# Seven half-size products in place of eight for the scan mixer's output projection, moved behind all four groups

## The chip, the cores and the metric

One core of a Trainium2 chip runs the whole program. The metric is the device time of one execution in microseconds (us); lower is better.

## The reference

A trunk of two layers on 1024 tokens of width 1024, all in float32. Layer 0 is windowed attention beside a pooling mixer, layer 1 is a Mamba-2 (SSD) mixer; a SwiGLU feed-forward network with 2816 hidden columns follows each. What the change touches is the end of the SSD mixer:

```python
y = ssd_chunked(xs, dt, A, Bm, Cm) + xs * D[:, None]        # 4 groups, 8 chunks of 128 tokens
y = y.reshape(b, s, 2048) * silu(z)                         # z = u @ w_in[:, :2048]
yg = y.reshape(b, s, 4, 512)
yg = yg * rsqrt(mean(yg * yg, -1) + EPS)                    # one mean for each token and group
y = yg.reshape(b, s, 2048) * norm_w
return y @ w_out                                            # 1024 x 2048 times 2048 x 1024
```

The result is added to the residual x, and `swiglu(rmsnorm(x))` comes next.

## The kernel before

The program is written by hand for each engine, in an order written out, with semaphores between the engines. PE is the matmul engine, DVE and POOL and ACT work on vectors, SP issues nearly all DMAs and waits in order.

**Matmul precision.** Each float32 product is three matmuls: an operand is split into a rounded part (`_hi`, copied by ACT) and the rest (`_lo`, a subtraction on DVE or POOL), and hi·hi, hi·lo and lo·hi are summed in a bank of PSUM. One such matmul has 128 rows of weights and 512 columns.

**Seven products.** The feed-forward layers, and the q stage that makes the inputs of the mixer, cut their matrices in four blocks and use seven block products (`M1` to `M7`) instead of eight, with sums of blocks made beforehand on DVE and POOL (`S1` to `S4`, `T1` to `T4`). The product that ends each FFN goes over slices: `down_slice(j, p)` is 12 matmuls for product j and row pair p; its operands come by DMA into a ring of 5 places (`s_val`, `d_val`), ACT makes the hi parts, POOL and DVE the lo parts, and `add_down` on DVE adds a finished bank to `xres` at one to four places.

**The SSD stage.** Four groups g, each of eight chunks c (`ssd_group`). Per chunk PE does `token_major` (a small product and transposes of rows read back from `conv_rows` into `bc_rows` and `yx`), `STATES`, `YOFF` and `YDIAG`; DVE masks the decays (`mdec`), updates the state and writes y into `yx`; ACT takes the exponentials; POOL scales (`xds`, `decayed`). Between chunks PE fills in `z_half` pieces (12 matmuls each, 16 in a group), which make the gate z. After the eight chunks the group's own output projection runs: y is multiplied by silu(z) (`gated`), squared, split in hi and lo with `norm_w` (`y_hi`, `y_lo`), and 16 outputs (8 token tiles, 2 column halves) of 4 row blocks each are computed with `out_part`, 192 matmuls. Since the mean is per token, and tokens lie on the partitions of the output, the factor 1/rms is applied by `add_out(rms)` on DVE when the bank is added to `xres`. The next group starts under the last outputs. In the last group the outputs go in the order `TILE_ORDER`, and the norm and the transposes (`ffn_T`) of the FFN behind are placed between them, tile by tile.

**FFN entry.** PE needs for its first products `M1g`, `M2g`, `M1u`, `M2u` only tiles 0 to 3; `M5g`, `M6g`, `M7g` need the block sums `T1`, `T2`, `T3` over tiles 4 to 7 (`tail_t1`, `tail_t2`, `tail_t3`, `tail_b22`, and then the lo parts `tail_lo1` to `tail_lo3` on DVE).

## Time and profile before

| | |
|---|---|
| median of 3 runs | 2283.26 us (2281.89 to 2283.43) |
| the profiled execution | 2282.14 us, of which the span of the trace is 2280.4 us |
| PE busy | 2258.5 us, 99% of the span |
| DVE, ACT, POOL busy | 1320.3, 1101.5, 1320.6 us |
| granted TensorE clock | 0.999 of full speed over the span |
| group of the SSD stage, scan and projection | 118.1 us |
| bytes by DMA | 281.45 MB, mean 123 GB/s |

Matmuls overlap, so a row's mean duration (390 ns for 128x512) is longer than the distance between two of them (227 ns); sums of PE work are made from distances.

### The profile page before, as it was taken

The page shows a single profiled execution, that of the slowest core. Times are in us where ns is not written, and L with a number is a line of the kernel's source. Part 1 is how long each engine was busy: PE and PEld are TensorE (multiplying, and loading weights), DVE is VectorE, ACT ScalarE, POOL GpSimd, SP SyncE. Part 2 cuts the span into 40 slices and gives each one's busy share as a digit, 9 for nine tenths or more (in the row PEclk, how much of TensorE's full clock was granted, in tenths as well). Part 3 has the DMA queues.
Part 4 walks back from the last instruction along what each step waited for, and adds up shares of the span by engine and source line. Part 5 has one row for each costly group of instructions (what it writes and reads, how often), then busy time and mean ns, then how long its engine had stood idle before and what let it go on. Part 6 is the DMA issues. An engine that isn't in the chain of part 4 may idle for free.

```text
span 2280.4 us, 28960 instructions
## 1 busy us (share of the span) xinstructions
PE 2258.5 (99%) x10698; PEld 1845.5 (81%) x10698; DVE 1320.3 (58%) x1716; ACT 1101.5 (48%) x2016; POOL 1320.6 (58%) x950
## 2 busy tenths in 40 slices
PE   8999999999999999999999999999999999999998
PEld 6877888888888878888878888888888888888887
DVE  7357663333335798855568484747854343336777
ACT  4046544333333446655567474737643333334445
POOL 3224288777774664787734242334388777774654
PEclk9999999999999999999999999999999999999999
DMA  5100323323227855233263323232222323228744
GB/s 164 47 28 19 120 64 112 120 88 120 88 102 259 268 161 166 93 112 119 86 222 123 120 84 118 86 102 93 102 88 97 122 84 122 85 106 292 250 148 155
DMA packets 170807, 281.45 MB, mean 123 GB/s; under 512 B 19232, under 2 KB 104108, under 8 KB 168108
## 3 DMA queue, kind: packets, MB, share of 16 engines
q1 hardware_dynamic: 167084, 267.68, 34.9%
q10 hardware_dynamic: 3584, 11.93, 1.3%
q8 instruction: 86, 1.41, 0.3%
q14 instruction: 53, 0.43, 0.1%
HBM read 209.71 MB, written 69.86 MB: 123 GB/s over the span
## 4 chain that ended last, share of the span: by engine, by line
PE 92%; DVE 3%; POOL 2%; issue 1%; ACT 1%; DMA 1%; SPq 0%; ACTq 0%; DVEq 0%; POOLq 0%
PE ps L2212 44%; PE ps L1925 8%; PE ps L1927 8%; PE ps L1926 8%; PE ps L2302 5%; PE ps L2306 5%; PE ps L2298 5%; PE ps L2592 1%; PE ps L2582 1%; PE ps L2575 1%; PE ps L1948 1%; PE ps L2370 1%; POOL sq L1205 1%; PE ps L2135 1%; PE ps L2168 1%
## 5 line engine op out<-in xcount | busy, mean ns | idle before, releaser
L1051 POOL TENSOR_TENSOR s_lo<-s_val,s_hi 128x512 fp32r<-128x512 f32 x154 | 235.5, 1533 | 196.7 <-ACT s_hi L1575 196.0
L2862 DVE TENSOR_TENSOR xres<-ps,xres 128x512 f32<-128x512 f32 x132 | 90.5, 688 | 400.2 <-PE ps L2212 400.2
L947 POOL TENSOR_TENSOR w_lo<-w_raw,w_hi 128x1024 fp32r<-128x1024 f32 x50 | 119.3, 2387 | 270.6 <-ACT w_hi L1239 205.9
L972 POOL TENSOR_TENSOR p_lo<-p_val,p_hi 128x512 fp32r<-128x512 f32 x176 | 239.4, 1369 | 48.6 <-ACT p_hi L1380 37.5
L1380 ACT ACTIVATE p_hi<-p_val 128x512 fp32r<-128x512 f32 x176 | 111.0, 632 | 307.8 <-POOL p_val L998 307.8
L2212 PE MATMUL ps<-xn_hi,p_hi 128*128 128x512 f32 x704 | 189.0, 390 | 1.2 <-ACT xres L1483 1.2
L2212 PE MATMUL ps<-xn_lo,p_hi 128*128 128x512 f32 x704 | 188.2, 389 | 0.0
L2212 PE MATMUL ps<-xn_hi,p_lo 128*128 128x512 f32 x704 | 188.2, 389 | 0.0
L1575 ACT ACTIVATE s_hi<-s_val 128x512 fp32r<-128x512 f32 x154 | 97.0, 630 | 160.8 <-DMA d_val<-in_w_down 89.9
L1925 PE MATMUL ps<-xn_hi,w_hi 128*128 128x512 f32 x400 | 160.3, 401 | 0.0
L1926 PE MATMUL ps<-xn_lo,w_hi 128*128 128x512 f32 x400 | 156.0, 390 | 0.0
L1927 PE MATMUL ps<-xn_hi,w_lo 128*128 128x512 f32 x400 | 155.9, 390 | 0.0
L2212 PEld LDWEIGHTS ps<-xn_hi,p_hi 128*128 128x128 f32 x704 | 131.5, 188 | 28.9 <-ACT p_hi L1380 2.0
L2212 PEld LDWEIGHTS ps<-xn_lo,p_hi 128*128 128x128 f32 x704 | 132.1, 188 | 27.5
L2212 PEld LDWEIGHTS ps<-xn_hi,p_lo 128*128 128x128 f32 x704 | 132.2, 188 | 27.5
L2302 PE MATMUL ps<-d_lo,s_hi 128*128 128x512 f32 x560 | 151.3, 390 | 1.0 <-DVE d_lo L2914 0.8
L2298 PE MATMUL ps<-d_hi,s_hi 128*128 128x512 f32 x560 | 151.0, 390 | 0.0
L2306 PE MATMUL ps<-d_hi,s_lo 128*128 128x512 f32 x560 | 150.7, 389 | 0.0
L2914 DVE TENSOR_TENSOR d_lo<-rows_v,d_hi 128x512 fp32r<-128x512 f32 x108 | 126.3, 1173 | 21.7 <-ACT d_hi L1578 21.6
L1483 ACT ACTIVATE xres<-ps 128x512 f32<-128x512 f32 x132 | 77.8, 591 | 113.8 <-PE ps L2212 113.8
L1239 ACT ACTIVATE w_hi<-w_raw 128x1024 fp32r<-128x1024 f32 x48 | 50.0, 1051 | 159.9 <-PE ps L1927 154.4
L2302 PEld LDWEIGHTS ps<-d_lo,s_hi 128*128 128x128 f32 x560 | 104.7, 188 | 24.6 <-DVE d_lo L2914 3.1
(361 smaller groups left out, 5570.3 us busy)
## 6 DMA issues: line engine op xcount, KB each, us to landing
s_val<-hidden SPq DMA_DIRECT2D x154, 256.0 KB, 2.9
hidden<-xres SPq DMA_DIRECT2D x20, 1792.0 KB, 6.5
wv_g<-in_w_gate SPq DMA_DIRECT2D x22, 1024.0 KB, 5.2
wv_u<-in_w_up SPq DMA_DIRECT2D x20, 1024.0 KB, 5.1
d_val<-in_w_down SPq DMA_DIRECT2D x70, 256.0 KB, 4.1
rows_v<-in_w_down SPq DMA_DIRECT2D x64, 256.0 KB, 3.8
mdec<-decay_sums SPq DMA_DIRECT2D x32, 512.0 KB, 4.2
xres<-parked_x SPq DMA_DIRECT2D x24, 512.0 KB, 6.0
```

Of the source, the lines that this page charges most:

```text
L947: pool.tensor_tensor(w_lo[piece.slot][:, :], raw[piece.raw][:, :], f(w_hi[piece.slot][:, :]), ALU.subtract).then_inc(lo_done, 1)
L972: pool.tensor_tensor(p_lo[n][:, :, :], src, f(p_hi[n][:, :, :]), ALU.subtract).then_inc(p_lo_done, 1)
L1051: pool.tensor_tensor(s_lo[i][:, :], s_val[i][:, :], f(s_hi[i][:, :]), ALU.subtract)\
L1380: act.activation(p_hi[n][:, :, :], src, ACT.Copy).then_inc(p_hi_done, 1)
L1925: pe.matmul(dst, l_hi, r_hi, start=first, stop=False, skip_group_check=reopened)
L1926: pe.matmul(dst, l_hi, r_lo, start=False, stop=False, skip_group_check=reopened)
L1927: return pe.matmul(dst, l_lo, r_hi, start=False, stop=last, skip_group_check=reopened)
L2212: ins = pe.matmul(bank, l_[:, k, :], r_[:, k, :], start=first and k == 0, stop=last and k == H2 - 1, skip_group_check=reopened)
L2298: pe.matmul(banks[t_], s_hi[i][:, t_ * P:(t_ + 1) * P], d_hi[i][:, :], start=p == 0, stop=False)
L2302: pe.matmul(banks[t_], s_hi[i][:, t_ * P:(t_ + 1) * P], d_lo[i][:, :], start=False, stop=False)
L2306: pe.matmul(banks[t_], s_lo[i][:, t_ * P:(t_ + 1) * P], d_hi[i][:, :], start=False, stop=False)\
L2914: dve.tensor_tensor(d_lo[i][:, :], down_operand(DOWN[j], p, i), f(d_hi[i][:, :]), ALU.subtract).then_inc(d_lo_done, 1)
```

## The change

The output projection of all four groups is taken out of the groups and done once behind the scans, as seven block products over 8 row pairs (56 slices, `out_slice`, 672 matmuls), in the manner of `down_slice`. For this:

- y must be normalized before the projection, since sums of blocks mix token halves. The squares are summed with the tokens along the free dimension (`square_sums` with the small matrix `pick`), ACT roots 4 rows, DVE inverts them, SP stores them to `rr_rows` and reads them back spread over all partitions (`root_row`), and DVE multiplies (`row_normed`). DVE then makes the block sums (`mix`, S1 to S4), and SP stores 14 blocks of 256 KB of each group to `gated_y` (`store_blocks`), from where `load_out` reads them slice by slice.
- This work of group g-1 stands inside the chunks of group g; that of the last group stands behind its scan. `yx` has two buffers. The rows of the next group are loaded in chunks 6 and 7 of the running one, and `token_major(k + 1)` runs across the border of groups.
- Two `z_half` pieces follow every chunk (in group 0, three stand ahead and one or two follow). No `out_slice` runs before the last scan ends. The order `OUT_SEQ` takes nine slices that don't need the last group first: six of M1 and three of M2.
- The residual x is read back from DRAM (`load_x_back`) and added with M1. The FFN entry of layer 1 is `second_entry`, with tiles in natural order: transposes of tiles 0 to 3 (`second_T`) between slices of M3, those of tiles 4 to 7 behind the projection.
- The q stage's semaphores are merged with those of the FFN products (names only).

The core of the diff, which stands for the same pattern elsewhere too:

```diff
+        OUT_SEQ = ([(0, p) for p in range(6)] + [(1, p) for p in range(3)] + [(0, p) for p in (6, 7)]
+                   + [(1, p) for p in range(3, NO)] + [(j, p) for j in range(2, 7) for p in range(NO)])
+        OUTS = len(OUT_SEQ)
...
+        Z_AFTER_CHUNK = [[(5,), (6, 7), (8,), (9,), (10, 11), (12, 13), (14,), (15,)],
+                         [(0, 1), (2, 3), (4, 5), (6, 7), (8, 9), (10, 11), (12, 13), (14, 15)],
+                         [(0, 1), (2, 3), (4, 5), (6, 7), (8, 9), (10, 11), (12, 13), (14, 15)],
+                         [(0, 1), (2, 3), (4, 5), (6, 7), (8, 9), (10, 11), (12, 13), (14, 15)]]
+        SILU_AFTER_CHUNK = [{1: (0, 1), 4: (2, 3, 4)}] + [{2: (0, 1), 4: (2, 3), 6: (4, 5)}] * (G - 1)
+        SILU_LATE = [(5, 6, 7)] + [(6, 7)] * (G - 1)
+        NEXT_PIECE = {6: 0, 7: 1}
+        LATE_PIECE = {0: 2, 1: 3}
...
+            def root_row(n):
+                sp.wait_ge(rms_ready, n + 1)
+                sp.dma_start(rr_rows[n], rinv[0:4, :]).then_inc(rr_stored, 16)
+                sp.wait_ge(rr_stored, 16 * (n + 1))
+                if n >= 2:
+                    sp.wait_ge(y_normed, BG * (n - 1))
+                if n:
+                    sp.wait_ge(rr_loaded, 16 * n)
+                sp.dma_start(rr[n % 2][:, :], rr_rows[n:n + 1].rearrange("a t l -> a (t l)").to_broadcast([P, BANK]))\
+                    .then_inc(rr_loaded, 16)
...
+                    if c == 6:
+                        if g:
+                            sp.wait_ge(y_normed, BG * 2 * g)
+                            store_blocks(g - 1, "M1", "M2")
+                            sp.wait_ge(mix_ready, 8 * (g - 1) + 4)
+                            store_blocks(g - 1, "M7")
+                        else:
+                            sp.wait_ge(gc_ready, 1)
+                        if not last:
+                            load_xrows(g + 1, 0)
+                            load_bc(g + 1, 0)
+                            load_piece(g + 1, 2)
+                    if c == 7:
+                        if g:
+                            sp.wait_ge(mix_ready, 8 * g)
+                            store_blocks(g - 1, "M6", "M3")
+                            sp.wait_ge(y_stored, 16 * 14 * g)
+                        if not last:
+                            load_xrows(g + 1, 1)
+                            sp.wait_ge(ydiag_full, NT * (g + 1))
+                            load_bc(g + 1, 1)
...
+            def out_loads(load_gate):
+                for s_ in range(2, 6):
+                    load_out(s_)
+                load_x_back(4)
+                load_out(6)
+                load_out(7)
+                load_x_back(0)
+                root_row(2 * G - 2)
+                load_x_back(5)
+                first_stores(G - 1)
+                sp.wait_ge(y_stored, 16 * (14 * (G - 1) + 4))
+                root_row(2 * G - 1)
+                load_out(8)
+                load_x_back(1)
+                sp.wait_ge(y_normed, BG * (2 * G - 1) + 2)
+                store_blocks(G - 1, "M1")
+                sp.wait_ge(y_stored, 16 * (14 * (G - 1) + 6))
...
+                load_out(9)
+                load_out(10)
+                load_x_back(6)
+                sp.wait_ge(y_normed, BG * 2 * G)
+                store_blocks(G - 1, "M2")
+                load_out(11)
+                load_x_back(2)
+                sp.wait_ge(mix_ready, 8 * (G - 1) + 4)
+                store_blocks(G - 1, "M7")
...
+            def square_sum(n):
...
+                        pool.wait_ge(m_ready, t.count("half", 2 * c + 2))
+                        lo(in_group(g + 1)(NEXT_PIECE[c]))
+                    if c == 1 and g:
+                        square_sum(2 * g - 1)
+                    if c == 5:
+                        square_sum(2 * g)
+                    if c >= 6 and g == G - 1:
...
+            def second_T(q):
+                pe.wait_ge(xn_ready, t.count("tile", 1))
+                if q < 2:
+                    pe.wait_ge(out_added, o_add_order.count(0, "M7", 2 * q + 1, 0, 1))
+                elif q == 4:
+                    pe.wait_ge(out_added, o_add_order.count(0, "M3", 1, 4, 1))
+                else:
+                    turn_free(1, {2: 0, 3: 1, 5: 2, 6: 4, 7: 5}[q])
+                transposed(turn_banks(1, q), xs_f[q % 2]).then_inc(turn_full, 1)
...
+            def out_slice(s_):
+                j, p = OUT_SEQ[s_]
+                n, i, banks = SLICES + s_ + 1, o_place(s_), out_banks(j)
+                if p == NO - 1:
+                    pe.wait_ge(s_lo_done, n)
+                    pe.wait_ge(d_lo_done, n)
+                    for t_ in range(4):
+                        mm3(banks[t_], os_hi[i][:, t_ * P:(t_ + 1) * P], os_lo[i][:, t_ * P:(t_ + 1) * P],
+                            od_hi[i][:, :], od_lo[i][:, :], False, True, True).then_inc(out_full, 1)
+                    return
+                pe.wait_ge(s_hi_done, n)
+                pe.wait_ge(d_hi_done, n)
+                for t_ in range(4):
+                    if p == 0 and j >= 2:
+                        pe.wait_ge(out_added, max(o_add_order.count(0, DOWN[j - 2], t_, first, half)
...
+                SUMS_AT = (3, 6) if last else (3, 7)
...
+                    if c in SUMS_AT:
+                        *first, final = Z_AFTER_CHUNK[g][c]
+                        for i in first:
+                            z_half(g, i)
+                        if c == 3 and g:
+                            square_sums(2 * g - 1)
+                        elif c == (6 if last else 7):
+                            square_sums(2 * g)
+                        z_half(g, final)
+                    else:
+                        for i in Z_AFTER_CHUNK[g][c]:
+                            z_half(g, i)
                 t.add("chunk", NT)
...
-                for n in range(2 * NT):
-                    if n == (2 * TILE_ORDER.index(4) if last else NT):
-                        pe.wait_ge(y_split, t.count("z", 2 * BG))
-                    out_part(n, [BG - 1] if n < EARLY_OUTS else range(BG)).then_inc(out_full, 1)
-                    if n in SSQ_AFTER_OUT[last]:
-                        square_sums(SSQ_AFTER_OUT[last].index(n))
-                    if last and n % 2 and n // 2 >= 2:
-                        ffn_T(1, n // 2 - 2)
-                t.add("z", 2 * BG)
...
+            for s_ in range(OUTS):
+                out_slice(s_)
+                if s_ == 3:
+                    square_sums(2 * G - 1)
+                if o_at(6, 2) <= s_ <= o_at(6, 5):
+                    second_T(s_ - o_at(6, 2))
...
+            def row_normed(g, b, h):
+                dve.wait_ge(rr_loaded, 16 * (2 * g + h + 1))
+                dve.wait_ge(sq_ready, BG * (2 * g + h + 1))
+                dve.scalar_tensor_tensor(half_of(g, b, h), half_of(g, b, h), gconst[:, g, GC_NW + b:GC_NW + b + 1],
+                                         rr[h][:, :], ALU.mult, ALU.mult).then_inc(y_normed, 1)
...
+                    masked_decay(c)
+                    if k + 1 < NT * G:
+                        token_major(k + 1)
+                    if c == 0 and g:
+                        gated(g - 1, 1)
+                        reciprocal_rms(2 * g - 2)
+                    if c == 2 and g:
+                        for b in range(BG):
+                            row_normed(g - 1, b, 0)
+                        for i in range(2):
+                            mix(g - 1, "S1", i)
+                    if c == 4:
+                        gated(g, 0)
+                        if g:
+                            reciprocal_rms(2 * g - 1)
+                    if c == 6 and g:
+                        for b in H1_ORDER:
+                            row_normed(g - 1, b, 1)
+                        for i in range(2):
+                            mix(g - 1, "S3", i)
+                    if c == 7 and g:
+                        for name in ("S2", "S4"):
+                            for i in range(2):
+                                mix(g - 1, name, i)
+                    if c >= 6 and last:
+                        out_low(c - 6)
...
+            gated(G - 1, 1)
+            reciprocal_rms(2 * G - 2)
+            out_low(2)
+            out_low(3)
+            for b in range(BG):
+                row_normed(G - 1, b, 0)
+            for i in range(2):
+                mix(G - 1, "S1", i)
+            out_low(4)
+            reciprocal_rms(2 * G - 1)
+            out_low(5)
+            for b in H1_ORDER:
+                row_normed(G - 1, b, 1)
+            for name in ("S3", "S2", "S4"):
+                for i in range(2):
+                    mix(G - 1, name, i)
+            ffn(1)
...
+                    for s_ in range(6, OUTS):
+                        j, p = OUT_SEQ[s_]
+                        if s_ + 1 < OUTS:
+                            out_sum(s_ + 1)
+                        if j == 6 and p in (5, 6):
+                            make(2 * p - 10)
+                            if p == 5:
+                                make(1)
+                        if (j, p) == (6, 7):
+                            make(3)
+                        out_low(s_)
...
+                            quota, limit = 8, "M1"
+                        elif j >= 2 and p in (0, 1):
+                            quota, limit = (4, "M1") if j == 2 else (0, "M1")
+                        elif 2 <= j <= 5 and p >= 3:
+                            quota, limit = 3, DOWN[j - 1]
+                        else:
+                            quota, limit = 0, "M1"
+                        for _ in range(quota):
+                            if taken < upto[limit]:
+                                add_result(*pending[taken])
+                                taken += 1
+                        if j == 6 and p in (3, 4):
+                            for t_ in (2 * p - 6, 2 * p - 5):
+                                add_result("M7", t_, 0, 0)
+                                add_result("M7", t_, 0, 1)
+                        if j == 6 and p >= 6:
+                            lo(p - 6)
...
+                    lo(2)
+                    lo(3)
+                    for t_ in range(4):
+                        add_result("M3", t_, 4, 1)
+                    for q in range(4, NT):
+                        make(q)
+                    for i in range(4):
+                        tail_t1(i)
+                        tail_t2(i)
+                        tail_t3(i)
+                        tail_b22(i)
+                    for i in range(4):
+                        tail_lo1(i)
+                    for i in range(4):
+                        tail_t4(i)
+                        tail_lo2(i)
+                    for i in range(1, 4):
+                        tail_lo3(i)
...
```

## Rows read from the trace of the kernel before

**Rows 1.** The page, part 1: busy us of each engine.

```profile
PE 2258.5 (99%) x10698; PEld 1845.5 (81%) x10698; DVE 1320.3 (58%) x1716; ACT 1101.5 (48%) x2016; POOL 1320.6 (58%) x950
```

**Rows 2.** Waits of PE over the span: us in total, times, longest.

```profile
PE ps L2606 <- POOL sq L1205: 1.6, 3, 0.5
```

**Rows 3.** Chain in order of time: token transposes of chunk 0, two groups.

```profile
1285.27 0.44 PE ps L2544 x4
...
1403.41 0.44 PE ps L2544 x4
```

**Rows 4.** PE timeline, FFN down projection of layer 0: one slice to the next.

```profile
858.31 1.07 PE L2298 MATMUL ps<-d_hi,s_hi 128*128 128x512 f32 x4
...
861.03 1.07 PE L2298 MATMUL ps<-d_hi,s_hi 128*128 128x512 f32 x4
```

**Rows 5.** PE timeline, one chunk of group 1, to the next chunk's start.

```profile
1324.27 0.38 PE L2537 MATMUL ps<-bc_rows 128*128 128x128 f32 x2
...
1326.88 1.09 PE L2592 MATMUL ps<-mdec,xdt 128*64 128x128 f32 x16
1333.47 0.38 PE L2537 MATMUL ps<-bc_rows 128*128 128x128 f32 x2
```

**Rows 6.** Busy us by window inside group 1's scan: PE, PEld, DVE, ACT, POOL.

```profile
1320.00:1340.00 20.00, 20.00 (x123) 16.26 (x122) 15.70 (x32) 14.54 (x35) 8.23 (x7) 1.00 0.32 99
```

**Rows 7.** Groups by line and shape on POOL, the same stretch.

```profile
L1205 POOL TENSOR_TENSOR sq<-sq,sq 128x512 f32<-128x512 f32 x6 | 9.3, 1543 | 16.9 <-ACT sq L1871 16.5
```

**Rows 8.** Timeline of SP's queue at a group's start: DMA issues.

```profile
1400.39 0.33 SPq L856 DMA_DIRECT2D mdec<-decay_sums  x1
...
1401.24 0.47 SPq L804 DMA_DIRECT2D yx<-conv_rows  x1
```

**Rows 9.** DMA issues, 1398 to 1408 us: KB each, us to landing.

```profile
yx<-conv_rows SPq DMA_DIRECT2D x1, 1024.0 KB, 7.5
...
bc_rows<-conv_rows SPq DMA_DIRECT2D x1, 512.0 KB, 5.4
```

**Rows 10.** DMA issues over the whole span: KB each, median us to landing.

```profile
s_val<-hidden SPq DMA_DIRECT2D x154, 256.0 KB, 2.9
...
d_val<-in_w_down SPq DMA_DIRECT2D x70, 256.0 KB, 4.1
...
conv_rows<-xres SPq DMA_DIRECT2D x24, 512.0 KB, 3.3
...
decay_sums<-sumT ACTq DMA_DIRECT2D x1, 128.0 KB, 2.4
```

**Rows 11.** DVE timeline, entry of the second FFN.

```profile
1649.09 0.68 DVE L2766 TENSOR_TENSOR t_val<-ps,comb_val 128x512 f32<-128x512 f32 x1
...
1651.60 0.68 DVE L2766 TENSOR_TENSOR t_val<-ps,comb_val 128x512 f32<-128x512 f32 x1
...
1653.40 1.28 DVE L2791 TENSOR_TENSOR xn_lo<-t_val,xn_hi 128x512 fp32r<-128x512 f32 x2
...
1658.81 4.81 DVE L2803 TENSOR_TENSOR comb_lo<-comb_val,comb_hi 128x512 fp32r<-128x512 f32 x3
```

**Rows 12.** DVE timeline, last product of layer 0's down projection.

```profile
889.20 2.47 DVE L2926 TENSOR_TENSOR xres<-ps,xres 128x512 f32<-128x512 f32 x4
...
894.77 1.56 DVE L2691 SCALAR_TENSOR_TENSOR xs_n<-xres,small,norm_wp 128x1024 f32<-128x1024 f32 x1
```

**Rows 13.** PE timeline, the same product: its first slice, the first transpose.

```profile
883.33 1.07 PE L2298 MATMUL ps<-d_hi,s_hi 128*128 128x512 f32 x4
...
896.93 1.04 PE L1948 MATMUL ps<-ident,xs_n 128*128 128x128 f32 x8
```

**Rows 14.** Busy us by window, layer 0's down projection (columns as in rows 6).

```profile
822.00:852.00 30.00, 29.25 (x125) 22.74 (x124) 30.00 (x32) 13.81 (x23) 19.78 (x12) 1.00 0.43 127
```

More of the change, by code:

```diff
@@ new lines, in ssd_group @@
+                for c in range(NT):
+                    if NT * g + c + 2 < NT * G:
+                        load_decay(NT * g + c + 2)
+                    if c == 0 and g:
+                        root_row(2 * g - 2)
+                    if c == 1 and not last:
+                        load_piece(g + 1, 0)
+                    if c == 2 and g:
+                        first_stores(g - 1)
+                    if c == 2 and not last:
+                        load_piece(g + 1, 1)
+                    if (g, c) == (0, 3):
+                        store_row(row_at(NQ - 1, "g", 1))
+                        store_row(row_at(NQ - 1, "g", 2))
+                    if c == 3 and last:
+                        load_out(0)
+                    if c == 4 and g:
+                        sp.wait_ge(y_stored, 16 * (14 * (g - 1) + 4))
+                        root_row(2 * g - 1)
+                    if (g, c) == (0, 5):
@@ L901, in ssd_group @@
[L901 to L906 removed]
+                    if c == 5 and last:
+                        load_out(1)
+                    if c == 6:
[10 more added lines that the diff above has]
+                            load_piece(g + 1, 2)
@@ L2222, in product @@
                         if mn == "M1g":
-                            turn_free(layer, 4)
+                            turn_free(layer, 3 if layer else 4)
+                        elif mn == "M1u" and layer:
+                            pe.wait_ge(out_added, o_add_order.count(0, "M3", 3, 4, 1))
                         elif mn == "M1u":
@@ new lines, in z_half @@
+            def z_half(g, i):
+                n = i // 2
+                u, (b, half) = ZU * g + n, Z_ORDER[g][n]
+                piece = in_group(g)(b)
+                if i % 2 == 0:
+                    if b not in [b_ for b_, _ in Z_ORDER[g][:n]]:
+                        pe.wait_ge(lo_done, piece.count(1))
+                    if u >= 3:
+                        pe.wait_ge(z_done, u - 2)
+                ins = columns(z_bank(u), piece, half, range(i % 2 * NK // 2, (i % 2 + 1) * NK // 2))
+                if i % 2:
+                    ins.then_inc(z_full, 1)
@@ new lines, in token_major @@
+            def token_major(k):
+                g, c = k // NT, k % NT
+                tok = slice(c * P, (c + 1) * P)
+                if c % 4 == 0:
+                    pe.wait_ge(rows_loaded[c // 4], 32 * (g + 1))
+                if k:
+                    pe.wait_ge(cb_freed, k)
+                if c == 5 and g:
+                    pe.wait_ge(rms_rooted, 2 * g)
+                elif c == 1 and g:
+                    pe.wait_ge(rms_rooted, 2 * g - 1)
+                ins = pe.matmul(ps[:, CB, 0:P], BT[:, tok], CT[:, tok], start=True, stop=True)
+                if c < NT - 1:
+                    ins = pe.transpose(ps[:, CB, P:2 * P], BT[:, tok], ident[:, :])
+                ins.then_inc(cb_full, 1)
+                if k:
+                    pe.wait_ge(xdt_ready, k)
+                for b in range(BG):
+                    ins = pe.transpose(ps[:, XS, b * P:(b + 1) * P], yx[g % 2][:, b, tok], ident[:, :])
+                ins.then_inc(xsT_full, 1)
@@ new lines, in square_sums @@
+            def square_sums(n):
+                pe.wait_ge(sq_summed, n + 1)
+                if n == 2 * G - 1:
+                    pe.wait_ge(ydiag_read, NT * G)
+                else:
+                    g = n // 2 + n % 2
+                    pe.wait_ge(cb_freed, NT * g + 5 if n % 2 else min(NT * (g + 1) + 1, NT * G))
+                for tt in range(4):
+                    ins = pe.matmul(ssq_rows(n), pick[:, 4 * tt:4 * tt + 4], sq[0][:, tt * P:(tt + 1) * P],
+                                    start=tt == 0, stop=tt == 3, skip_group_check=True)
+                ins.then_inc(ssq_full, 1)
```

1178 lines of the change are left out of this document (681 added, 497 removed), and 2 rows, old and new, of the table comb_hi_order.

## The prediction

> **What bounds the kernel now.** I read the page's busy shares first: PE is busy 99% of the span, the others 48% to 58% [rows 1]. Busy time counts overlapping matmuls, so the next view was the list of waits: at the group ends of the SSD stage PE waits only 1.6 us in all, for POOL's sum of squares [rows 2]. The timeline then gives PE's real rate: a slice of 12 matmuls comes every 2.72 us (858.31 to 861.03), so one matmul costs 0.2267 us [rows 4]. The chain in order of time gives the group: 1403.41 - 1285.27 = 118.14 us [rows 3]. The reader is to see that PE is the bound everywhere and that there is nearly no slack: what PE no longer does is won, and every wait put in front of it is lost. So the question is whether the new order still hides its dependences.
>
> **What is removed.** The projection falls from 4 x 192 = 768 matmuls to 56 x 12 = 672: 96 x 0.2267 = 21.8 us off PE, at the same form of matmul, so I give this term no other bounds. The group ends, now without a stop between scan and projection, give back the 1.6 us of [rows 2] and little more; I take 2 us (0 to 4: a group's matmuls, 384 x 0.2267 = 87.1, and eight chunks of 9.20 - 24 x 0.2267 = 3.76 us, 30.1 [rows 5], leave about 1 us of the 118.1). Transposes and z pieces stay as many. Gain: 24 us.
>
> **Cost A, the border between groups.** `token_major(k + 1)` now stands at the head of chunk 7 and wants the next group's rows. SP issues them in chunk 6, behind `load_decay(8g + 8)`, which waits for chunk 6's YDIAG. Behind that YDIAG PE has two z pieces, 24 x 0.2267 = 5.4 us, and then nothing. Before, the same trio (mdec, bc_rows, yx) took from 1400.39 to 1401.24 + 7.5 = 1408.7, 8.35 us [rows 8, 9]. So group 0 costs 2.9 us. In groups 1 and 2 SP waits longer, for four `row_normed` and two `mix` of the group before. From chunk 6's start DVE comes to them at about 1.8 us (an estimate: PE's transposes end at 1.0 and `xdt` takes one operation more), six operations take 0.6 us each when alone (1.28 for two) and 1.6 when POOL is active (4.81 for three) [rows 11]; at 0.9 they end at 7.2. Six stores go out meanwhile, some 0.35 us of issue each [rows 8], then the rows: issued at about 8.5, behind 1.5 MB of stores, landed at about 15.2. PE is there at 9.2 [rows 5]: 6 us, twice. A = 2.9 + 12 = 15 us (10 to 20, with the operations at 0.6 and 1.6 us). Queued behind PE's wait is all of chunk 7, and DVE, ACT and POOL wait with it, so they don't make up for it.
>
> **Cost B, the start of the projection.** Count from chunk 7 of group 3. PE: YDIAG to 3.5, two z pieces to 8.9, then slices at 2.72 and one `square_sums` of 0.9; unhindered it needs the DVE part of slice 6 (`out_low(6)`) at 8.9 + 0.9 + 6 x 2.72 + 0.9 = 27. What has to happen before, since DVE keeps its order and SP its own: masks and four mixes (5.5); four stores issued (7) and landed, 3.3 us [rows 10] (10), for which SP waits; 14 loads issued at 0.33 to 0.47 us [rows 8] (15.4), whose 4 MB arrive, at the pace of [rows 8, 9] less one latency, by 22 to 23; behind them in the same queue the first `rr_rows` store and its load back, 2.4 to 2.9 us each [rows 10] (25.6); four `row_normed`, two mixes (30.5); four stores and their landing (35); the second `rr_rows` store and load (40.2); then `row_normed` x4 and `mix` x6 at 0.7 us (47) and only then `out_low(6)` (47.7). Slice 4 waits on the way for the first half of the chain, which changes nothing of the end. B = 47.7 - 27 = 21 us. Low end, every DMA at 2.4 and every operation at 0.6: 15. High end, 4.1 (the slice loads of [rows 10]) and 1.6: 28. Slice 9 needs M1's last stores, back at about 50 and wanted at 55: hidden behind slices 6 to 8.
>
> A DMA's landing in [rows 10] runs from 2.4 us for 128 KB to 4.1 for 256 KB in a busy queue. The Trainium skill, "DMA: Bandwidth & Descriptors", section "Anatomy of one DMA — SWDGE (gpsimd) path", says that each DMA pays about 2.0 us fixed besides its bytes at 436 GB/s. It speaks against this change, which strings seven dependent DMAs before slice 9; by it (an estimate from that page) they cost 14 us fixed, and B would be near its low end, where the traces' prices give 21.
>
> **Cost C, the FFN entry.** Three places. First, `second_T(0)` stands behind slice 3 of M3, 8.2 us after its start. In layer 0 the like transpose stood five slices behind, 883.33 to 896.93, with no wait [rows 13]; DVE made the M7 adds from 5.9 us on, and the norm began 11.4 us after the start and took 1.56 [rows 12, 13]. The adds stand one slice earlier now; the norm ends at about 12: 4 us. Second, T6 follows T5 on PE directly, but needs the banks of T4, and DVE frees these (four operations, 1649.09 to 1651.60 = 2.5 us [rows 11]) only after `make(7)` (1.3 us), which waits for T5: 4 us. Third, from there DVE has 3 x 2.5 us more of such sums, four `tail_lo1`, eight of `tail_t4` and `tail_lo2` (0.6 alone), then three at 1.6; PE has M1u, M2u and one transpose between, 6.3 us, and M5g and M6g wait for their low parts: 4 us (1 to 9). Before, outputs stood between the tiles and this work was hidden; now only products of tiles 0 to 3 cover it. C = 12 us (8 to 17).
>
> **Cost D, DVE and POOL inside the scans.** A scan lasts 8 x 9.2 = 73.6 us of PE. DVE was busy 15.70 of 20 us there [rows 6], 58 us a scan, and gets 16 operations more: 10 us at 0.6, 26 at 1.6. So it lies between 68 and 84 of 73.6: hardly hidden. POOL's sum of squares (3 x 1.54 = 4.6 us [rows 7]) now stands ahead of `xds` of chunk 2, about 1 us too late. In the projection, slices with sums, low parts and three adds fill DVE wholly; in layer 0 such a stretch cost PE 0.75 of 30 us [rows 14]. I take 4 us together (0 to 20), near the low end, since the waits of A give DVE time to catch up.
>
> [Rows 11] show 0.6 us for a DVE subtraction from SBUF alone and 1.6 beside POOL. The Trainium skill, "SBUF — State Buffer", section "SBUF: two separate sides", calls the pair of ports shared by the two an exclusive lock held for a whole instruction. If that struck all 16 operations, DVE would be the bound of the scans, which is the third rival.
>
> **Sum.** -24 + 15 + 21 + 12 + 4 = +28 us on the profiled span of 2280.4: 2308.4. That execution took 2282.14, 1.7 us beside its span, and the median of the runs is 1.1 above it: 2311 us. With the ends of the terms the four costs are 33 to 85 us and the gain 22 to 26, so the time lies between 2290 and 2346 if the mechanisms hold; I take the middle of most, since their ends are independent and none of the rows favours one side.
>
> **Rivals.** (1) All is hidden and PE stays the bound: 2283.3 - 24 = 2259 us. For it: [rows 2] show a kernel whose order hides its waits; PE has 33 us of work from the last YDIAG to slice 9. Against: nothing stands on PE behind the z pieces at the group border. It decides if A, B, C and D together stay under 24 us, which asks above all that the chain of B fit into 27 us. Chance 0.10. (2) B is hidden, because small DMAs overtake the bulk loads and DVE's order fits; A, C and D remain: 2283.3 + 7 = 2290. Chance 0.15. (3) DVE becomes the bound of the scans, 84 instead of 73.6 us in the three groups with the new work: 2311 + 3 x 10 = 2341. Chance 0.07. That fewer matmuls are not run is no rival: the loops count them.
>
> **Numbers.** My forecast, all four costs, has 0.68, with a range of its own of 2297 to 2326. What a measurement can tell here from no change is 0.2%, 4.6 us. Rival 1 and its edge give faster 0.12; the edge between rivals 1 and 2 gives same 0.05; slower 0.83. The range, 2288 to 2329, holds rival 2 and leaves out rivals 1 and 3 and the tails.
>
> **What would show it.** In the trace of after: 672 matmuls in the projection; PE idle before the transposes of `yx` (or the product before them) once in each of groups 0 to 2, released by the row DMAs, 3, 6, 6 us; PE idle in the early slices, released by DVE's low parts, some 20 us in all; idle before three to four matmul groups and transposes at the FFN entry, released by DVE, 12 us; DVE above 85% in the scans. I am wrong if the rows are landed when chunk 7 begins, or if DVE reaches `out_low(6)` before PE has done slice 5.

## The result

Median after 2365.2 us (2363.2 to 2367.9, 4 runs), before 2282.9 (2281.9 to 2283.4, 4 runs beside them): ratio 1.0362, 95% interval 1.0344 to 1.0380. The change costs 82 us. The prediction had the direction (slower, 0.83) and far too little of it: 2311 us, with 2329 as the upper end.

### The profile page after: what moved, and what is told of

It is laid out like the page before. It is cut to its first block, busy times and chain, and to the rows that moved or that the text cites. A ratio compares the mean times of both kernels' runs of the same rounds, so it can differ in the third digit from the quotient of the medians.

```text
span 2366.2 us, 29286 instructions
## 1 busy us (share of the span) xinstructions
PE 2267.5 (96%) x10602; PEld 1842.8 (78%) x10602; DVE 1425.7 (60%) x1828; ACT 1147.5 (48%) x2101; POOL 1369.6 (58%) x992
## 4 chain that ended last, share of the span: by engine, by line
PE 84%; DVE 7%; DMA 3%; issue 2%; POOL 2%; SPq 1%; ACT 1%; DVEq 0%; ACTq 0%; POOLq 0%
PE ps L2525 43%; PE ps L2228 5%; PE ps L2230 5%; PE ps L2229 5%; PE ps L2617 5%; PE ps L2621 5%; PE ps L2613 5%; PE ps L2909 1%; PE ps L2913 1%; PE ps L2905 1%; PE ps L2251 1%; PE ps L2974 1%; PE ps L2694 1%; DVE yx L3791 1%; DMA bc_rows<-conv_rows 1%
## 5 line engine op out<-in xcount | busy, mean ns | idle before, releaser
L1143 POOL TENSOR_TENSOR w_lo<-w_raw,w_hi 128x1024 fp32r<-128x1024 f32 x34 | 81.7, 2406 | 197.3 <-ACT w_hi L1471 114.6
L2525 PE MATMUL ps<-xn_hi,p_hi 128*128 128x512 f32 x704 | 190.8, 393 | 1.9 <-ACT xres L1765 1.3
L2525 PE MATMUL ps<-xn_lo,p_hi 128*128 128x512 f32 x704 | 189.7, 392 | 1.4 <-DVE xn_lo L3145 1.4
L2525 PE MATMUL ps<-xn_hi,p_lo 128*128 128x512 f32 x704 | 188.2, 389 | 0.0
L2525 PEld LDWEIGHTS ps<-xn_lo,p_hi 128*128 128x128 f32 x704 | 133.2, 189 | 29.7 <-DVE xn_lo L3145 1.8
L2525 PEld LDWEIGHTS ps<-xn_hi,p_hi 128*128 128x128 f32 x704 | 132.6, 189 | 30.2 <-ACT p_hi L1616 3.1
L2525 PEld LDWEIGHTS ps<-xn_hi,p_lo 128*128 128x128 f32 x704 | 132.3, 188 | 27.6
L1397 POOL TENSOR_TENSOR os_lo<-os_val,os_hi 128x512 fp32r<-128x512 f32 x56 | 89.6, 1607 | 104.7 <-ACT os_hi L2135 104.6
L2617 PEld LDWEIGHTS ps<-d_lo,s_hi 128*128 128x128 f32 x560 | 104.7, 188 | 25.6 <-DVE d_lo L3331 4.2
```

Of the source, the lines that this page charges most:

```text
L2525: ins = pe.matmul(bank, l_[:, k, :], r_[:, k, :], start=first and k == 0, stop=last and k == H2 - 1, skip_group_check=reopened)
L2617: pe.matmul(banks[t_], s_hi[i][:, t_ * P:(t_ + 1) * P], d_lo[i][:, :], start=False, stop=False)
```

## The profile after

The page of the kernel after, parts 1 and 2 (busy us; then the granted clock in 40 slices), beside [rows 1]:

```profile
span 2366.2 us, 29286 instructions
PE 2267.5 (96%) x10602; PEld 1842.8 (78%) x10602; DVE 1425.7 (60%) x1828; ACT 1147.5 (48%) x2101; POOL 1369.6 (58%) x992
...
PEclk9999999999999999999999899889989999999999
```

The 96 matmuls are gone (10698 to 10602). PE's idle time rose from 2280.4 - 2258.5 = 21.9 us to 2366.2 - 2267.5 = 98.7, by 76.8. And its busy time rose by 9.0 us although 21.8 us of work had left it. The last row says why: the clock, 0.999 over the span before and 0.982 now, shows an 8 in four slices from the 23rd to the 30th. So there are two things to read here: the waits, and what they do to the clock.

PE's waits in the kernel after, from the first scan to the first products behind the projection (us in total, times, longest), beside [rows 2]:

```profile
PE ps L2864 <- DMA bc_rows<-conv_rows: 20.6, 3, 7.6
PE ps L2909 <- DVE od_lo L3747: 16.9, 2, 9.4
PE ps L2974 <- DVE mdec L3835: 10.7, 7, 2.1
PE ps L2905 <- DVE xres L3761: 7.4, 3, 3.1
PE ps L2525 <- DVE comb_lo L3151: 7.2, 1, 7.2
PE ps L2251 <- DVE xn_lo L3135: 4.1, 1, 4.1
PE ps L2957 <- POOL xds L1426: 2.6, 3, 0.9
```

L2864 is `token_major` (cost A), L2905 and L2909 are `out_slice` (B), L2525 and L2251 products and `second_T` (C), L2974 and L2957 YDIAG and STATES in the scans (D). With the smaller rows they are 20.6, 27.2, 16.5 and 13.3 us, 77.6 in all.

The same kernel by windows: four in a row around one wait for rows, then one stretch of lowered clock each in the scans, in the projection and at the FFN entry (PE, PEld, DVE, ACT, POOL busy, granted clock, DMA share, GB/s):

```profile
1227.00:1232.00 5.00, 5.00 (x37) 3.87 (x35) 3.87 (x10) 2.78 (x6) 0.49 (x1) 1.00 0.38 84
1232.00:1235.34 3.34, 0.04 (x1) 0.00 (x0) 0.47 (x1) 1.54 (x6) 2.34 (x1) 1.00 0.95 325
1235.34:1242.17 6.83, 4.30 (x23) 4.08 (x25) 1.87 (x4) 3.33 (x7) 1.04 (x1) 0.50 0.49 167
1242.17:1250.00 7.83, 7.83 (x60) 5.80 (x57) 4.92 (x11) 5.92 (x8) 1.53 (x1) 1.00 0.73 252
...
1392.35:1395.77 3.42, 3.42 (x10) 2.68 (x9) 3.35 (x9) 3.11 (x5) 1.64 (x2) 0.50 0.41 153
...
1542.54:1552.78 10.24, 5.86 (x14) 4.65 (x15) 7.34 (x12) 2.36 (x5) 8.63 (x3) 0.50 0.77 236
...
1716.62:1723.45 6.83, 5.17 (x17) 4.42 (x18) 6.57 (x11) 4.09 (x8) 1.27 (x1) 0.50 0.42 173
```

PE stops at 1232, the clock goes from 2.4 to 1.2 GHz at 1235.3 while it is still idle, PE starts again at 1237.9, and full clock comes back at 1242.2. In between 4.3 us of work ran at half speed; about 2.2 of them are lost behind a wait of 5.8. There are eleven such stretches, 78.6 us, with PE busy for 50.7 of them: half of that, 25.3 us, is lost. By place: rows 14.0 us busy, so 7.0 lost; scans 10.3 and 5.1; projection 16.3 and 8.2; entry 10.1 and 5.0. The Trainium skill, "TensorE: Matmul & The Clock Gate", section "What's actually happening", calls the halved clock the default that activity releases; the rows agree with its two levels and with its direction.

The sum on the spans: -21.8 (matmuls) + 76.8 (idle) + 25.3 (clock) = +80.3; measured 85.8. About 2.0 of the other 5.5 us are the eight `square_sums`, which have a new form: PE takes 1.29 us from the last z matmul ahead of one to the first behind it (1281.96 to 1283.25), where the sums of before took 1.03 (1596.79 to 1597.82). The last 3.5 us are not explained. They are not a matter of the waits: PE's busy time less half of its work at the lower clock is 2241 to 2244 us in the traces of all 14 kernels behind the change (in e3_fill less the 20.4 us of its fill), whether PE stood for 58 us or for 103.

PE's timeline at the start of the projection (start, us, instruction, in brackets the idle time before it and its releaser):

```profile
1531.87 2.07 PE L2909 MATMUL ps<-od_lo,os_hi 128*128 128x512 f32 x4 [9.40 <-DVE od_lo L3747]
...
1546.92 2.08 PE L2909 MATMUL ps<-od_lo,os_hi 128*128 128x512 f32 x4 [7.55 <-DVE od_lo L3747]
...
1584.32 0.79 PE L2905 MATMUL ps<-od_hi,os_hi 128*128 128x512 f32 x1 [3.10 <-DVE xres L3761]
```

DVE at the same place:

```profile
1525.55 4.34 DVE L3802 SCALAR_TENSOR_TENSOR yx<-yx,gconst,rr 128x512 f32<-128x512 f32 x4 [8.79 <-DMA rr<-rr_rows]
...
1539.92 2.74 DVE L3802 SCALAR_TENSOR_TENSOR yx<-yx,gconst,rr 128x512 f32<-128x512 f32 x4 [6.70 <-DMA rr<-rr_rows]
```

And SP's queue:

```profile
1515.22 0.50 SPq L939 DMA_DIRECT2D rr_rows<-rinv  x1
1521.56 0.33 SPq L945 DMA_DIRECT2D rr<-rr_rows  x1
```

The low part of slice 4 stands on DVE behind the first four `row_normed`, which wait for the row's round trip: stored at 1515.2 behind 14 loads, back at 1525.5. That is the first wait; slice 6's is the second; M1's adds, which DVE reaches late, the third.

## The experiments

Each is the kernel after with one edit, unless it says otherwise. Differences are of medians; by the intervals of the ratios such a difference is uncertain by some 5 us, so for the small ones (e8, e6, and e1, whose highest run is as slow as the kernel after) the waits in the trace carry the verdict.

**e3_fill: the clock alone.**

```
+ if c == NT - 1 and not last:
+     pe.wait_ge(xdt_ready, k + 1)
+     for _ in range((26, 32, 32)[g]):
+         pe.matmul(ps[:, XS, :], xn_hi[:, 0, 0:P], xn_hi[:, 0, 0:BANK], start=True, stop=True)
  token_major(k + 1)
```

> At the three borders between groups TensorE is idle for the rows for 5.8, 7.2 and 7.6 us. Here 26, 32 and 32 matmuls of the z pieces' form (0.2267 us each, 5.9, 7.3 and 7.3 us) run in that wait, into the bank that the transposes write next; their result is overwritten, and nothing of the computation is left out. Theory (a wait costs its own length and then half of the work that runs at the lower clock after it): the granted clock stays at 1.0 there; in the three stretches at half clock TensorE was busy for 4.57, 6.35 and 3.92 us, half of it comes back, 7.4 us: 2358 us (2355 to 2361). Rival (after the wait DVE, ACT or DMAs set the pace, so the clock costs nothing): 2365 us, with the clock at 1.0 all the same. Second rival (the clock does not depend on TensorE's idle time): the three stretches stay at half clock, 2365 us or more.

2359.1 us, 6 less (7.4 expected), ratio 1.0326 (1.0311 to 1.0341). By windows:

```profile
1232.00:1238.00 6.00, 5.29 (x27) 4.17 (x26) 0.05 (x1) 4.89 (x11) 1.61 (x1) 1.00 0.92 327
1238.00:1245.00 7.00, 7.00 (x56) 5.84 (x55) 5.10 (x12) 3.51 (x6) 1.04 (x1) 1.00 0.47 147
```

The rows come when they came before, PE has nothing more useful to do, and the kernel is faster: the clock stays at 1.00 at all three borders. The wait's second price is real. Its size at the borders is less sure, since more changed than was aimed at: in this trace two of the three short stretches in the scans are gone too, with the same waits for masks (10.7 us), and 24 us of PE's work ran at the lower clock where after had 50.7.

**e2_rows_pe and e1_rows_sp: cost A from PE's side and from SP's.**

```
  # PE (and DVE, behind the y sums)
- if k + 1 < NT * G: token_major(k + 1)                  # head of every chunk
+ if k + 1 < NT * G and c < NT - 1: token_major(k + 1)
+ ... z_half(g, 14); if c == NT - 1 and not last: token_major(k + 1); square_sums(2 * g); z_half(g, 15)
```

> The first token_major of the next group is moved from the head of chunk 7 to behind its YDIAG and first z piece, on TensorE and on DVE (behind the y sums). SP's order is unchanged, so the rows land as before, 5.8 to 7.6 us after chunk 7 begins; TensorE comes to them at 3.8 + 2.7 = 6.5 us. Theory (cost A is a wait with nothing in front of it, plus the clock): of 20.6 us idle 2 remain, and 7.4 us of half clock go too; up to 1 us a border for DVE's copies before the sum of squares comes on: 20.6 - 2 + 7.4 - 3 = 23 us less, 2342 us (2338 to 2348). Rival (the wait moves: xds and states of chunk 0 are late by what token_major is later): 2355 to 2365 us, idle before STATES and YDIAG of chunk 0.

```
+ if c == 5 and not last: load_bc(g + 1, 0)
  if c == 6: wait y_normed, mix_ready
-     store M1, M2, M7; load_xrows(g + 1, 0); load_bc(g + 1, 0)
+     load_xrows(g + 1, 0); store M1, M2, M7
```

> SP's order alone: the B and C rows of the next group are issued in chunk 5, and the x rows in chunk 6 ahead of the stores of M1, M2 and M7 instead of behind them. Theory of the prediction (rows are behind six stores' issue, 2.1 us, and their 1.5 MB, in groups 1 and 2, and behind DVE's row_normed and mixes, which stay): the waits for rows fall from 20.6 to about 12 us, the clock gives back 3: 2354 us (2349 to 2359). Rival (DVE's operations ahead of the stores are all of it): waits stay at 17 or more, 2361 us or more. In group 0, which has no stores, both expect 1 us or so, since only the B and C rows come earlier.

e2 2347.9 us, 17 less (23 expected); e1 2358.5, 7 less (11). In e2's waits of PE the rows fell from 20.6 to 6.8, of which group 0 alone has 5.0: `Z_AFTER_CHUNK` gives it one piece behind chunk 7 and not two, so the moved `token_major` has none in front of it there. The masks took some back:

```profile
PE ps L2974 <- DVE mdec L3837: 14.0, 9, 2.1
...
PE ps L2864 <- DMA bc_rows<-conv_rows: 6.8, 3, 5.0
```

e1's waits for rows fell to 13.8. So two things are shown to set cost A, how much work stands ahead of PE's wait, and SP's stores ahead of the loads, the first for more.

**e4_spread and e8_spread_pool: cost D.** DVE's new operations in halves over two chunks:

```
- if c == 0 and g: gated(g - 1, 1); reciprocal_rms(2 * g - 2)
+ if c == 0 and g: gated(g - 1, 1, (0, 1)); reciprocal_rms(2 * g - 2)
+ if c == 1 and g: gated(g - 1, 1, (2, 3))
  ... likewise row_normed over chunks 2 and 3, gated(g, 0) over 4 and 5
```

> DVE's added operations inside the scans are halved over two chunks: gates in chunks 0 and 1 and in 4 and 5, row_normed in 2 and 3, the first stores in chunk 3. The number of operations is the same. Theory (cost D is lumps of 4 to 6 us ahead of a mask, not too much work in all: DVE is idle 6 us at every border and 3 us in chunks between): waits of YDIAG and STATES fall from 13.3 to about 4 us, and the three stretches of half clock beside them (3.41 us each, all busy) give back 5: 2351 us (2347 to 2356). Rival (DVE is the bound of the scans): the waits only move, 2362 us or more.

2371.6 us, 6 more. The theory failed; PE's waits in the scans show where the time went:

```profile
PE ps L2957 <- POOL xds L1426: 15.2, 3, 5.1
PE ps L2974 <- DVE mdec L3835: 0.6, 1, 0.6
```

The mask waits went as expected. But POOL's `square_sum` of chunk 1 now waited for the gates of chunk 1, and behind it in POOL's queue stood `xds` of chunk 2. e8 moves it (`- if c == 1 and g: square_sum(2 * g - 1)`, `+ if c == 2 and g: ...`).

> e4_spread again, and POOL's sum of squares of the second half moved from chunk 1 to chunk 2, behind its xds. In e4_spread the 10.7 us of waits for masks fell to 0.6, and 15.2 us of waits for xds came, 5.1 us once in each of groups 1 to 3, where POOL stood in the sum of squares and waited for the gates that now come in chunk 1. Theory (D is lumps in DVE's and POOL's order, not too much work): both kinds of wait go, under 3 us stay, 10 us less idle than after and 5 us less of half clock: 2350 us (2346 to 2355). Rival (DVE has too much work, the wait finds another place): 2360 us or more.

2361.2 us, 4 less than after and 10 less than e4: the xds waits are gone, but three mask waits of 2.7 us (8.0 us) are there, as the rival had it (2360 or more, the wait finds another place). DVE's timeline ahead of one:

```profile
1350.80 5.72 DVE L3899 SCALAR_TENSOR_TENSOR yx<-yx,gconst,eacs 128x128 f32<-128x128 f32 x4
1356.44 2.35 DVE L3835 TENSOR_TENSOR mdec<-mdec,cbm 128x512 f32<-128x512 f32 x2
```

POOL's:

```profile
1355.06 4.87 POOL L1405 TENSOR_TENSOR sq<-sq,sq 128x512 f32<-128x512 f32 x3
```

The four y sums take 5.72 us here.

**e11_small_sums: is it POOL?** e8_spread_pool with `- sq[0][:, :]`, `+ sq[0][:, 0:8]` in POOL's sums, which leaves the squares of most columns out.

> e8_spread_pool with POOL's sums of the squares made over 8 of 512 columns, so that the norm is not the reference's; left out are 21 POOL operations of 1.5 us. In the trace of e7_all, which has the same order, the four y sums beside these POOL operations took 5.72 us instead of 1.14. Theory (the mask waits of 2.7 us in each of groups 1 to 3 come from POOL holding DVE up, not from the number of DVE's operations): 8.5 us of waits fall to under 1.5, 3 us of half clock go with them: 2361 - 10 = 2351 us (2347 to 2355), and the y sums there take 1.2 to 2 us. Rival (DVE's own lumps make the wait): 2358 us or more.

2352.8 us, 8 less than e8 (10 expected); the mask waits fell from 8.0 to 1.8. The part on the y sums was wrong:

```profile
1344.86 4.71 DVE L3899 SCALAR_TENSOR_TENSOR yx<-yx,gconst,eacs 128x128 f32<-128x128 f32 x4
1349.49 1.28 DVE L3835 TENSOR_TENSOR mdec<-mdec,cbm 128x512 f32<-128x512 f32 x2
...
1355.85 1.14 DVE L3899 SCALAR_TENSOR_TENSOR yx<-yx,gconst,eacs 128x128 f32<-128x128 f32 x4
```

The y sums still took 4.71 us, beside POOL's `w_lo`, `xds` and `decayed`; what the sums of squares had added is 1.0 us there and 1.1 on the masks. In the next chunk, with POOL idle, they took 1.14. The sums of squares were enough to make the waits, but they are only a part of what POOL does to DVE.

**e9_mask_first: the mask ahead of the y sums.** `masked_decay(c + 1)` moves on DVE in front of chunk c's y sums.

> After, with one move on DVE: the mask product of chunk c + 1 stands ahead of the four y sums of chunk c instead of behind them; nothing else changes. Theory (D: DVE is only late at the mask that YDIAG waits for, by lumps of at most 2.1 us that the y sums of 1.1 to 5.7 us can take instead): the 10.7 us of waits for masks fall under 3, xds stays at 2.6, and half of the three stretches of 3.4 us at half clock comes back: 2365 - 8 - 5 = 2352 us (2348 to 2358). Rival (the mask product then waits for ACT's exponentials, or ACT waits for the y sums): 2363 us or more.

2355.5 us, 10 less (13 expected): mask waits 10.7 to 3.2, xds 2.6 to 1.5. Alone it is the best repair of D, and its trace has no stretch of lowered clock in the scans but those behind the waits for rows.

**e5_proj: cost B.**

```
- OUT_SEQ = [(0, 0..5), (1, 0..2), (0, 6), (0, 7), (1, 3..7), ...]
+ OUT_SEQ = [(0, 0..5), (1, 0..5), (0, 6), (0, 7), (1, 6), (1, 7), ...]
  # SP: rr_rows stored ahead of load_out(6), load_out(7); load_out(8) ahead of first_stores
  # DVE: out_low(4) ahead of the first row_normed, out_low(5) to out_low(11) between the norm's operations
```

> The start of the projection: twelve slices of groups 0 to 2 instead of nine come ahead of the first that needs the last group; the row of reciprocal roots is stored before the loads of slices 6 and 7, slice 8 is loaded ahead of the second row's round trip, and DVE splits slices 4 to 11 between the norm's operations instead of behind all of them. The work is the same. Theory (cost B is the order, DVE's low part of slice 6 and the loads of 8 and up behind the chain): of 27.2 us of waits between 1515 and 1610 us some 6 stay (slice 12 some 2 us late, slice 14 and the adds another 4), and of the three stretches at half clock (17.1 us busy in them, 8.6 lost) 7 come back: 2365 - 28 = 2337 us (2331 to 2345). Rival (the chain of seven dependent DMAs is longer than any cover, and the wait moves to slice 12): 2350 us or more.

2358.4 us, 7 less where 28 were expected; the rival (2350 or more) holds. PE's waits of the projection:

```profile
PE ps L2238 <- DVE od_lo L3757: 9.4, 2, 7.5
PE ps L2915 <- DVE xres L3771: 5.1, 2, 3.1
```

From 27.2 only to 20.2 us. The wait moved to slice 15: DVE makes its low part behind the sum of slice 16, and SP loaded slice 16 behind the last stores' landing.

**e6_entry: cost C.** DVE's order: `make(7)` behind the tails of tile 4, three `tail_t4` ahead of `tail_lo1`.

> DVE's order at the FFN entry alone: the sums of tile 4 come before the norm of tile 7 instead of behind it, and three of the four T4 subtractions (1.75 us each beside POOL) move from in front of the low parts that M6g waits for into the gaps before and between the tiles. Theory (cost C is order): T6's wait of 4.1 us goes, M6g's of 7.2 us falls to 2, and of the 5.3 us that the two stretches at half clock cost 4 come back: 2352 us (2348 to 2357). Rival (DVE's work between M3's adds and M6g's low parts is the bound, in whatever order): M6g waits as much longer as T6 waits less, 2362 us or more.

2359.7 us, 5 less (13 expected): waits 16.5 to 12.0. T6's 4.1 fell to 0.5, but M5g now waits 2.4 and 3.1 for parts that came late, M6g 2.8. DVE is busy without a gap from M3's adds to M6g's low part, so both were half right: the order mattered for 4 us, the rest is DVE's work.

**e7_all, e10_all2, e12_all3: together.** e7 is e1, e2, e8, e5 and e6, with group 0's x rows in chunk 5 too; e10 adds e9 and loads slices 16 and 17 ahead of the wait for the last stores; e12 has those loads without e9.

> All together: the rows' loads ahead of the stores and the first token_major behind a z piece (in group 0 the x rows in chunk 5 too), the spread gates and norms with POOL's sum behind xds, the projection's start and the FFN entry. Theory (the four costs are independent waits in TensorE's order, each with its half clock): rows 28 us, scans 15, projection 28, entry 13, together 84 of the 82 us: 2283 us (2275 to 2296), the granted clock 1.0 but for one or two stretches, TensorE idle under 35 us. Rival (the costs share DVE, and what one gives the next takes): 2305 us or more.

> e7_all with the mask product ahead of the y sums, and with the loads of slices 16 and 17 ahead of the wait for the last stores. In e7_all 12.3 us of waits for masks, 3.1 us for the sum of squares behind the rows and 8.4 us for the low part of slice 15, which DVE makes behind the sum of slice 16, were left. Theory: masks under 3 us, slice 15 under 2, and 7 us of half clock: 2327 - 9 - 7 - 7 = 2304 us (2298 to 2312), still slower than before, with the entry and DVE's pace beside POOL left. Rival (DVE is the bound of the scans in this order): 2318 us or more, with waits of the same sum elsewhere.

> e7_all with the loads of slices 16 and 17 ahead of the wait for the last stores, and without the mask product's move, which made e10_all2 slower by making DVE wait 25.1 us for ACT's exponentials. Theory: of e7_all's 8.4 us for the low part of slice 15, which DVE makes behind the sum of slice 16, 4 go, and 4 us of half clock in the projection; the adds' waits stay: 2327 - 7 = 2320 us (2315 to 2325). Rival (the loads only move the wait to the adds): 2326 us or more. No theory has it faster than before (2283).

e7 2327.5 us, e10 2337.8, e12 2323.0: ratios 1.0196, 1.0241 and 1.0187 (1.0171 to 1.0203). e7 missed its forecast of 2283 by 45 us and e10 its 2304 by 34; both lie where their rivals put them. e12 is in its range, but its five runs reach from 2322.6 to 2330.2 and e7's four from 2326.1 to 2330.2, so that it is faster than e7 isn't shown. The single repairs give 7 + 17 + 4 + 7 + 5 = 40 us, e7 38. So e7's rival had the number, but hardly the reason: the gains add up, and what is missing was missing in each repair alone, which together gave under half of the 90 us of their expectations. It is no proof that the costs are independent (e7 has one edit more, and e1 and e2 go for the same wait), and e9 shows that they are not wholly so, since it stops paying there. Waits of DVE in e10's scans:

```profile
DVE mdec L3859 <- ACT mdec L2187: 25.1, 12, 4.0
```

In e9 this was 14.7 us, and there PE stood for rows for 21.6 us, in which the others could catch up; that this hid it is my reading, which no run isolates. No version beats the kernel before: e12 is 40 us behind it. Its PE is idle for 2321.2 - 2258.7 = 62.5 us, 40.6 more than before, and 33.5 us of its work ran at half clock, 16.7 lost: 40.6 + 16.7 - 21.8 = 35.5 of the 40.8 on the spans.

**e13_light_dve: is it DVE?** e12 with `row_normed` and POOL's sums over 8 columns in the scans.

> e12_all3 with row_normed over 8 of 512 columns in groups 0 to 2 and POOL's sums of squares over 8 of 512, so that the norm is left out for most columns; DVE is spared 24 operations of 0.65 to 1.2 us and POOL 24 of 1.5. Theory (in the best order DVE, busy for 218 of 235 us of the scans in e7_all, is the bound there): the waits for masks and for DVE's copies, 15.4 us, fall under 3, with the half clock of the scans (6.8 us): e12_all3 less 15 us, 2305 us (2300 to 2311). Rival (the order, ACT or the DMAs bound the scans): at most 5 us less than e12_all3.

2317.1 us, 6 less than e12: nearer the rival's 5 than the theory's 15. Most columns stay without the norm here, and both DVE and POOL are spared. The scans by window, of e12:

```profile
1245.00:1480.00 235.00, 220.73 (x1326) 174.97 (x1325) 215.29 (x344) 183.40 (x364) 102.83 (x67) 0.97 0.43 147
```

and of e13:

```profile
1245.00:1480.00 235.00, 226.73 (x1367) 180.08 (x1366) 192.99 (x356) 184.82 (x367) 74.85 (x68) 0.99 0.46 156
```

DVE falls from 92% busy to 82% and PE gains 6 us: the mask waits go (12.3 to 2.7 us), while DVE waits 16.0 us for ACT and PE 7.1 instead of 3.1 at the borders. So DVE, with POOL beside it, was the nearest bound of the best order, and ACT comes right behind it; which of the two mattered more, e13 doesn't separate.

## Why the prediction failed

| term | forecast | waits measured (gain: matmuls) | lost to the clock |
|---|---|---|---|
| gain | -24 | -21.8 | |
| A, borders | 15 (10 to 20) | 20.6 | 7.0 |
| B, start of projection | 21 (15 to 28) | 27.2 | 8.2 |
| C, FFN entry | 12 (8 to 17) | 16.5 | 5.0 |
| D, scans | 4 (0 to 20) | 13.3 | 5.1 |
| sum | +28 | +56 | +25 |

The four mechanisms were right: the main waits are at the places and from the engines that were named, and the repairs of each gave time back. The sum failed at two steps, and either alone would have left the measured time above the stated 2329: with the waits as measured and no clock it comes to some 2339 us, with the waits as forecast and the clock to some 2336.

**A term was missing.** The sum priced a wait at its length. The clock before was 0.999, since PE never stood for more than 1.6 us in all at these places [rows 2], so none of the rows showed what a stop does; that was a reason to ask, not to leave it out. The trace of before does hold one fall of the clock, at its very end, where it costs nothing: PE's last matmul ends at 2273.1 us, and from 2276.5 on the granted clock is 0.50. The clock took 25 us, nearly a third of the result; e3_fill shows that it is paid for the stop itself.

**All four costs were too small, D by three times.** Each lies in the upper half of its range or just above it. "I take the middle of most, since their ends are independent" failed with them: four ends that are missed on the same side add up.
- A: in groups 1 and 2 the forecast gave 6 us each, measured 7.2 and 7.6; the rows were issued at 1317.53, 9.2 us into chunk 6, where I had 8.5. Group 0 was forecast at 2.9 and took 5.8. The DMAs were not the reason: from the issue of `mdec` at 1229.16 to the landing at 1237.8 they took 8.6 us, forecast 8.35. The step that failed is "PE has two z pieces" behind chunk 6: that is so in groups 1 and 2, but `Z_AFTER_CHUNK` gives group 0 one piece there, 12 matmuls of 2.7 us, and 8.35 - 2.72 = 5.6.
- B: the chain itself was forecast to within 1 us. Counted from chunk 7 of group 3 (1499.47), the first row was back at 26.1 us (forecast 25.6), the second at 40.5 (40.2), and `out_low(6)` began at 46.7 (47). Slice 6 waited 7.55 us behind slice 4's 9.40, 17 together; the rest of the 21 is that PE came to slice 6 late, having waited and run at the lower clock on the way. What was missing stands beside the chain: M1's adds, which DVE does late, stopped PE for 7.4 us more, and three small waits for 2.9.
- C: T6 4.1 us as forecast (4); the low parts 9.2 (4 forecast, 1 to 9 given), since three of the four T4 subtractions took 1.75 us beside POOL and not 0.6 (the fourth, 0.68, came when POOL was idle); the transposes of tiles 0 to 3, 3.2 (4).
- D: 13.3 for 4. "I take 4 us together, near the low end, since the waits of A give DVE time to catch up" is the step that failed: the 0.6 or 1.6 us of one operation were right, but I counted DVE's sum over a scan, where PE waits for one mask in one chunk. Lumps of four operations ahead of a mask, and y sums of up to 5.7 us beside POOL, cost each chunk by itself.

PE's timeline at the border of group 0, from the first to the last matmul of its one z piece, and to the rows:

```profile
1228.99 0.50 PE L2228 MATMUL ps<-xn_hi,w_hi 128*128 128x512 f32 x1
...
1231.66 0.39 PE L2230 MATMUL ps<-xn_hi,w_lo 128*128 128x512 f32 x1
1237.87 0.80 PE L2864 MATMUL ps<-bc_rows 128*128 128x128 f32 x2 [5.82 <-DMA bc_rows<-conv_rows]
```

Rivals 1 (all hidden, 2259) and 2 (B hidden, 2290) are out. Rival 3 named DVE as the bound of the scans: not in the kernel after, where it was 81% busy (190.0 of 235 us); in the repaired one nearly so. The gain was right in its main term; that group ends give back 2 us can't be seen, and the `square_sums` took as much more.

## What to carry to other kernels

Where an engine is 99% busy, price a new wait at its length and then at half of the work that follows until the clock is back: here 77 us of waits cost 102. Count a helper engine by the piece of work that the bound engine waits for next, not by its sum over a stage, and look at what stands behind each moved operation in all queues, POOL's and SP's too. Read the first pass of a loop by itself: group 0 has another schedule than the rest, and a price made for the others missed half of its wait. A change that takes 1% of the matmuls away has to hide every new dependence: even with five repairs, this one stayed 1.9% slower.

## What the runs showed of the hardware

- In the kernel after, each single stop of PE of 4.1 to 9.4 us came with a fall of the granted clock to half for 6.8 to 10.2 us, and stops of 1.5, 3.1 and 2.8 us close together with one of 10.2. In the scans, beside waits of 2.1 us, it fell three times for 3.4 us. But such a short wait doesn't always bring it: e2_rows_pe has nine waits for masks, up to 2.1 us, and its clock is 1.00 from 1245 to 1500 us; e3_fill has the same waits as after and one such fall. Fill matmuls in a long stop kept the clock at 1.00 (e3_fill).
- Four DVE operations of 128x128 from SBUF took 1.14 us alone, 4.71 beside POOL's `w_lo`, `xds` and `decayed`, and 5.72 with its sums of squares as well. The Trainium skill, "SBUF — State Buffer", section "SBUF: two separate sides", calls the port pair of the two an exclusive lock for an instruction; the rows agree with that for operations with two inputs in SBUF, and show how far short operations can be stretched, to five times their length.
- A round trip through DRAM (`rr_rows`: a store of 2 KB, then a load of 256 KB) took 6.3 and 4.0 us behind 14 loads. The other seven in the same trace took at most 1.2 to 1.9 us for the store, and 3.0 to 3.4 for the load; the second one of the projection is 1535.34 to 1536.51 and 1539.9. The Trainium skill, "DMA: Bandwidth & Descriptors", section "Anatomy of one DMA — SWDGE (gpsimd) path", which the prediction quotes with 2.0 us fixed for each DMA, gives that figure for DMAs that GpSimd issues. SP issued these, and seven of the eight stores stay below it.
